# Attention scores over 128 rows: the low parts of the keys in their own tiles, padded with zeros

## The reference

```python
# first block, 8 heads
z = jnp.einsum('bhqd,bhkd->bhqk', q_blk, k_c) * scale
...
# second block, 16 heads
s = jnp.einsum('bhqd,bhkd->bhqk', q[:, :, lo:hi], k[:, :, :hi]).astype(jnp.float32) * scale
```

## Time and profile before

| | |
|---|---|
| median of 3 runs | 2132.58 us (2129.17 to 2135.8) |
| profiled execution, its own time | 2129.67 us |
| its span in the profile | 2127.9 us |
| mean granted TensorE clock | 0.992 |
| PE busy | 2082.2 us, 98% |
| DVE busy | 1106.3 us, 52% |
| ACT busy | 808.9 us, 38% |
| POOL busy | 111.9 us, 5% |

### The profile page before, as it was taken

How to read it: one execution, slowest core, us unless ns; L and a number is a source line. 1 busy time by engine, 2 the same in 40 slices (tenths; PEclk the granted TensorE clock), 3 DMA queues, 4 the chain that set the end, 5 groups by cost and what they waited for, 6 DMA issues and landing times.

```text
span 2127.9 us, 25125 instructions
## 1 busy us (share of the span) xinstructions
PE 2082.2 (98%) x10227; PEld 1720.3 (81%) x10227; DVE 1106.3 (52%) x1678; ACT 808.9 (38%) x1256; POOL 111.9 (5%) x131
## 2 busy tenths in 40 slices
PE   6999999999999999999999999999999999999997
PEld 4788888887778888888888887777888888888887
DVE  8734444576744554333335546564524476446546
ACT  4422222354544333222234445555323354234334
POOL 3100000100000010000011000000000100000012
PEclk8999999999999999999999999999999999999999
DMA  7734543443332313232222332222233222332241
GB/s 277 268 135 154 177 142 123 142 139 119 124 104 89 98 62 118 75 111 102 87 82 91 109 119 70 70 70 74 96 93 96 89 80 87 102 109 92 79 147 40
DMA packets 70165, 236.27 MB, mean 111 GB/s; under 512 B 7826, under 2 KB 10130, under 8 KB 69667
## 3 DMA queue, kind: packets, MB, share of 16 engines
q1 hardware_dynamic: 67874, 226.59, 32.2%
q0 software_dynamic: 2032, 7.90, 1.1%
q10 hardware_dynamic: 144, 0.18, 0.1%
HBM read 229.89 MB, written 4.75 MB: 110 GB/s over the span
## 4 chain that ended last, share of the span: by engine, by line
PE 92%; DVE 4%; ACT 2%; DMA 1%; issue 1%; POOL 0%; DVEq 0%; SPq 0%; ACTq 0%
PE bank L608 81%; PE bank L672 4%; PE bank L782 1%; PE bank L779 1%; PE bank L1012 1%; PE bank L894 1%; PE bank L998 1%; DVE w_lo L1570 1%; DVE raw_m L1566 0%; DMA w_raw<-in_w_mix_dram 0%; PE bank L924 0%; DVE kl L1759 0%; PE bank L987 0%; DVE ssq L1586 0%; PE bank L1044 0%
## 5 line engine op out<-in xcount | busy, mean ns | idle before, releaser
L1570 DVE TENSOR_TENSOR w_lo<-w_raw,w_hi 128x1024 fp32r<-128x1024 f32 (+2 forms) x367 | 418.2, 1167 | 217.0 <-ACT w_hi L1109 216.0
L608 PE MATMUL bank<-u_lo,w_hi 128*128 128x512 f32 (+1 forms) x1920 | 497.2, 371 | 11.2 <-DVE u_lo L1850 4.9
L608 PE MATMUL bank<-u_hi,w_hi 128*128 128x512 f32 (+1 forms) x1920 | 500.2, 373 | 6.7 <-ACT ple_s L1287 3.5
L608 PE MATMUL bank<-u_hi,w_lo 128*128 128x512 f32 (+1 forms) x1920 | 495.4, 371 | 0.0
L1109 ACT ACTIVATE w_hi<-w_raw 128x1024 fp32r<-128x1024 f32 (+2 forms) x368 | 347.4, 976 | 259.9 <-PE bank L608 195.5
L608 PEld LDWEIGHTS bank<-u_lo,w_hi 128*128 128x128 f32 x1920 | 357.1, 189 | 75.7 <-DVE u_lo L1850 5.7
L608 PEld LDWEIGHTS bank<-u_hi,w_hi 128*128 128x128 f32 x1920 | 358.9, 190 | 70.9 <-ACT ple_s L1287 3.9
L608 PEld LDWEIGHTS bank<-u_hi,w_lo 128*128 128x128 f32 x1920 | 357.2, 189 | 61.0 <-issue 2.3
L1688 DVE TENSOR_TENSOR ff_a<-ff_s,bank 128x512 f32<-128x512 f32 x44 | 30.2, 687 | 233.0 <-issue 220.2
L1183 ACT ACTIVATE act_hi<-ff_a 128x512 fp32r<-128x512 f32 x66 | 41.7, 632 | 256.7 <-DVE ff_a L1688 216.7
L608 PE MATMUL bank<-act_hi,w_lo 128*128 128x512 f32 (+1 forms) x561 | 131.1, 378 | 0.0
(11 more groups left out here) (270 smaller groups left out, 2126.4 us busy)
## 6 DMA issues: line engine op xcount, KB each, us to landing
w_raw<-in_w_gu_dram SPq DMA_DIRECT2D x127, 512.0 KB, 4.0
w_raw<-in_w_ada_dram SPq DMA_DIRECT2D x66, 512.0 KB, 4.5
w_raw<-in_w_dn_dram SPq DMA_DIRECT2D x48, 384.0 KB, 3.1
w_raw<-in_w_mix_dram SPq DMA_DIRECT2D x36, 512.0 KB, 3.6
w_raw<-in_w_dn_dram SPq DMA_DIRECT2D x48, 320.0 KB, 3.2
w_raw<-in_w_in_dram SPq DMA_DIRECT2D x24, 512.0 KB, 3.5
w_raw<-in_w_o_dram SPq DMA_DIRECT2D x16, 512.0 KB, 3.5
w_raw<-in_w_in_g_dram SPq DMA_DIRECT2D x16, 512.0 KB, 3.5
```

The lines of the kernel that those rows point to most:

```text
L608: m = e.matmul(bank[b][:, c], w, (x.lo if part == 2 else x.hi)[:, k, c], start=start, stop=stop, skip_group_check=True)
L1570: e.tensor_tensor(lo_of(name), raw_of(i), f32(hi_of(name)), ALU.subtract).then_inc(*s_w_lo.inc(name))
```

## The change

Each head of a pair gets its own tile for the low part of the keys (`kl_t[ph][s][p]`, eight tiles in all, four for each attention). The head's own 64 partitions are written by DVE as before; the other 64 are set to zero once for each attention by POOL (`zero_keys`). The second score product then reads the whole `qs` tile and the whole `kl` tile, 128 rows each: the rows in which `qs` holds the low part of the queries meet zeros. TensorE waits for the zeros (`s_kl_zero`) before a head's first product. To make room, `cv_y` is gone: the convolution accumulates in `yc_f` itself, and `cv_v` moves.

```diff
@@ tiles
-    kl_t = [ar(f"kl{s}", [P, T], F32R, 10 * s + 8) for s in range(2)]
+    kl_t = {ph: [[ar(f"kl{ph}{s}{p}", [P, T], F32R, 2 * s + at if p else 10 * s + 8) for p in range(2)] for s in range(2)]
+            for ph, at in (("a", 80), ("b", 44))}
...
-    cv_v = ar("cv_v", [P, T + 2], F32, 80)
-    cv_y = ar("cv_y", [P, T], F32, 82.5)
+    cv_v = ar("cv_v", [P, T + 2], F32, 84)
@@ TensorE
         def score(ph, out, c, p, queries, keys, keys_on_rows, start, stop):
-            s, own = c % 2, slice(64 * p, 64 * p + 64)
+            s = c % 2
+            q.wait_ge(s_kl_zero, (ph, s, p))
             q.wait_ge(s_q, (ph, c, 1))
             q.wait_ge(s_k, (ph, c, 1))
             a, k = qs_t[s][p][:, queries], ks_t[s][p][:, keys]
             l, r = (k, a) if keys_on_rows else (a, k)
             e.matmul(out, l, r, start=start, stop=False, skip_group_check=True)
-            a, k = qs_t[s][p][own, queries], kl_t[s][own, keys]
+            k = kl_t[ph][s][p][:, keys]
             l, r = (k, a) if keys_on_rows else (a, k)
             return e.matmul(out, l, r, start=False, stop=stop, skip_group_check=True)
@@ ScalarE, convolution
-                e.activation(cv_y[:, :], cv_v[:, 2:T + 2], ACT.Copy, scale=vec("conv_w", 8 + c)).then_inc(*s_cvy.inc(c))
+                e.activation(yc_f[:, c, :], cv_v[:, 2:T + 2], ACT.Copy, scale=vec("conv_w", 8 + c)).then_inc(*s_cvy.inc(c))
@@ VectorE, keys
-                e.tensor_tensor(kl_t[s][own, :], psum(key)[own, :], f32(ks_t[s][p][own, :]),
+                e.tensor_tensor(kl_t[ph][s][p][own, :], psum(key)[own, :], f32(ks_t[s][p][own, :]),
@@ VectorE, convolution
-                    e.scalar_tensor_tensor(cv_y[:, :], cv_v[:, k:k + T], vec("conv_w", 4 * k + c), cv_y[:, :], ALU.mult,
+                    e.scalar_tensor_tensor(yc_f[:, c, :], cv_v[:, k:k + T], vec("conv_w", 4 * k + c), yc_f[:, c, :], ALU.mult,
...
-                e.tensor_tensor(yc_f[:, c, :], cv_y[:, :], psum(key)[:, :], ALU.mult).then_inc(*s_yc.inc(c))
+                e.tensor_tensor(yc_f[:, c, :], yc_f[:, c, :], psum(key)[:, :], ALU.mult).then_inc(*s_yc.inc(c))
@@ GpSimd
+        def zero_keys(ph, key):
+
+            q.wait_ge(s_out, (key, 1))
+            for s in range(2):
+                for p in range(2):
+                    other = slice(64 - 64 * p, 128 - 64 * p)
+                    e.memset(f32(kl_t[ph][s][p][other, :]), 0.0).then_inc(*s_kl_zero.inc((ph, s, p)))
+                    q.wait_ge(s_kl_zero, (ph, s, p))
...
         last_squares("n1")
+        zero_keys("a", "1d17")
...
             add_square("n3", d, fold=True)
+        zero_keys("b", "2d17")
```

More of the change, by code:

```diff
@@ L352, in block_kernel @@
     arena = (cat + 63) // 64 * 64
-    assert base + arena + 86 * KB <= nc.sbuf_usable_end, base + arena + 86 * KB - nc.sbuf_usable_end
+    assert base + arena + 86 * KB + 32 <= nc.sbuf_usable_end, base + arena + 86 * KB - nc.sbuf_usable_end
     def ar(name, shape, dt, kb):
@@ L515, in block_kernel @@
     s_q_hi, s_q, s_k_hi, s_kl, s_k = signal("s_q_hi"), signal("s_q"), signal("s_k_hi"), signal("s_kl"), signal("s_k")
+    s_kl_zero = signal("s_kl_zero")
     s_v_act, s_v_dve = signal("s_v_act"), signal("s_v_dve")
```

## The result

The changed kernel takes 2107.47 us (median of 4 runs, 2105.64 to 2108.74), the kernel before 2131.39 (4 runs, 2129.17 to 2135.8, those shown above among them). The ratio is 0.9881, with a 95% interval of 0.9866 to 0.9896: 24 us, or 1.2%, faster. The forecast was 2108.5. The profiled execution took 2107.84 us, with a span of 2106.0 and a mean granted clock of 0.991.

What follows compares the result with a forecast made beforehand. PE was taken as the bound: 98% busy, 92% of the chain. 11.1 + 17.9 - 3.1 - 1.0 - 0.8 = 24.1 us saved, from the median 2132.58 to 2108.5 us; own range 2102 to 2114, chance 0.80.

Steps and rivals of the forecast that it cites:

- Phase a, 11.1 us: Phase a score bursts: seven heads save 1.47 us each, the first, which waits for `v_a`, 0.8; sum 11.1 us.
- Phase b, 17.9 us: Phase b score products: 64 steps save a mean of 0.28 us each, 17.9 us before anything is given back.
- Given back, 3.1 + 1.0 us: Phase b: 11 steps in five stretches off PE turn 3.1 us into wait; other turns with little slack, 1 us.
- POOL's zeros, 0.8 us: Boundaries before both phases: POOL's memsets may slow DVE's new input, so PE waits 0.4 us more at each.
- A: Phase b gives back 10 us instead of 4.1: 2114; with 2 us at each boundary 2118; chance 0.09.
- B: Score loads still wait because two products use the same rows; nothing saved, 2132.6 plus up to 2; chance 0.03.
- C: Score products: the switch is only half of the late load's cost, so 12 us are saved, 2120; chance 0.06.
- D: Half-clock stretches at phase b's 12 tiles and phase a's heads cost 34 us, 2142; decides from 14; chance 0.02.
- What would have shown the prediction wrong: Phase a bursts still over 2 us, phase b saving less than 10, or boundaries growing by over 1 us each.
- The dense layers kept 0.23 us from start to start: Sign in the profile after: matmuls of the dense layers still start 0.23 us apart.

Runs made afterwards that it cites:

- the kernel before with late low parts: Kernel before, with DVE writing the dense gate's low parts in phase b behind the next step's attention work: 2130.58 us, ratio 0.9983.
- the changed kernel with late low parts: Changed kernel, with DVE writing the dense gate's low parts in phase b behind the next step's attention work: 2102.45 us, ratio 0.9852.
- the grouped one: Kernel before, phase a's eight products per head reordered: four over 128 rows, then four over 64: 2124.57 us, ratio 0.9949.
- the third experiment: Kernel before, phase a's row-count switches cut from eight to two per head by reordering products, none widened: 2124.57 us, ratio 0.9949.

## Why the prediction was right

**Phase a, 11.1 us.** Measured 11.35, with a burst of 1.28 us where 1.26 was forecast. The pace of the sticks was the right row for a product not yet in the trace: same widths, same format, 128 rows. The other seven heads gained 1.48 us each, 10.36 in all (forecast 7 x 1.47 = 10.3). The first head gained 1.0 us, with a wait that grew by 0.28 us in it, where 0.8 was forecast, so nearly all of the term's error lies there.

**Phase b, 17.9 us.** Taken step by step, from the first score product to the second matmul after the mask, in the starts of the same matmuls, 64 steps save 17.35 us: 0.23 each with 128 columns (forecast 0.24), 0.28 with 256, 0.29 with 384 and with 512 (forecast 0.29). The term was 3% too large: each width saves up to 0.01 us less than forecast, and the mean of the four forecasts, 0.2775, had been rounded up to 0.28.

**Given back, 3.1 + 1.0 us.** 17.35 - 13.09 = 4.26 us, forecast 4.1; 3.56 of it stand as waits of PE, where about 4 were forecast. The size was right, but the picture behind it was only half so. I counted 11 score steps in five stretches off PE and let their saving turn into waits, which treats the stretches as fixed. They grew instead, from 37 to 67 us in all, since a shorter PE makes more of the steps depend on DVE. That the sum fits is in part luck: the return hangs in part on DVE's order of work, and moving 1.2 us of it took the return from 4.26 to 2.86 (17.35 - 14.49).

**POOL's zeros, 0.8 us.** The timeline of POOL before phase b, and the matmul that answers the earlier trace rows:

```profile
1140.88 2.25 POOL L2169 MEMSET klb<- 64x512 f32 x4 [5.36 <-PE bank L609]
```

```profile
1143.44 0.38 PE L609 MATMUL bank<-u_lo,w_hi 128*128 128x256 f32 x1 [1.00 <-DVE u_lo L1613]
```

Four memsets take 2.25 us. That is nearer to the memset of the earlier trace rows than to the sum of the earlier trace rows, as chosen. PE's wait grew from 0.88 to 1.00 us there, and from 0.49 to 0.72 before phase a, which looks like 0.35 us for the zeros. But the wait goes with the half-clock stretch at the boundary, not with the zeros. Before phase a it is 0.72 us in all five profiles with a stretch there and 0.49 in all four without. The first line below is of the kernel before with late low parts, which has no zeros; the second is of the changed kernel with late low parts, which has them:

```profile
425.92 0.39 PE L608 MATMUL bank<-u_lo,w_hi 128*128 128x256 f32 x1 [0.72 <-DVE u_lo L1615]
```

```profile
421.98 0.39 PE L609 MATMUL bank<-u_lo,w_hi 128*128 128x256 f32 x1 [0.49 <-DVE u_lo L1617]
```

Before phase b, in profiles without a stretch there, the wait is 1.00 us with zeros and 0.98 and 1.00 without (the kernel before with late low parts, and the grouped one). DVE's operations beside the memsets are no longer than in the kernels without zeros either: `ssq` takes 0.43 us, `hres` 0.48 to 0.49 and `u_lo` 0.42 to 0.48 in both kinds. So the zeros cost at most 0.02 us at a boundary, and the term of 0.8 was too large by all of it. Its reason, that POOL's writes might slow DVE, did not come about. No product waited for a zero.

**The rivals.** A did not come: 4.3 us were given back and not 10, and the zeros cost the boundaries nothing, not 4 us. B fell with the loads of the second head, which go ahead over the same 128 rows, against the rule quoted with it (the Trainium skill, TensorE: Matmul & The Clock Gate, Part 3: Packing small matmuls): here the trace disagrees with it. C fell with the result, 23.9 us and not 12; and the third experiment, with six switches fewer in each of eight heads, gives 8.03 / 8 / 6 = 0.17 us for each, near the 0.20 of the forecast, not half of it. D asked for 14 half-clock stretches; phase b has none, before or after, and its longest wait is 1.3 us.

What would have shown the prediction wrong did not come about: bursts under 2 us, phase b above 10, boundaries below 1. The dense layers kept 0.23 us from start to start. The errors were +0.25 us in phase a, -0.55 in the steps of b, -0.16 in the return and +0.8 in the zeros; they partly cancel and give the 24.4 us of the two phases, where 24.1 was forecast. Against the medians 23.9 us were gained. That this lies within 0.2 us of the forecast is luck too, since the interval of the ratio alone is 3 us to either side.

## What to carry to other kernels

Look in the loads' timeline for idle time that ends in "issue", not only at the matmuls: a load that goes out with its own matmul marks a switch, and in phase a each switch of the row count cost 0.17 to 0.20 us. Compare the load's start with its matmul's as well: behind products of 128 and 256 columns the idle time before a late load was only 0.07 to 0.13 us, and the view marks none of them. Remove switches by making the narrow product as wide as its neighbours with zeros, or, with no further tile, by grouping products of one row count (70% of phase a's gain). When PE gets shorter, read next what the engine behind its first wait does ahead of it, and move what is not urgent behind: here that was worth another 5 us, 3.65 of which could have been had in the kernel before.

## What the runs showed of the hardware

- A product over 64 rows is not slow by itself, and its loads go ahead when the product before has 64 rows too: four in 0.58 us. From the start of the last 128-row product with 512 columns to the first 64-row product, recorded with its bare load, it was 0.32 us, where 0.23 is the pace without a switch.
- The load of a bf16 product behind an fp32r product goes out late even though both use 128 rows, after 0.28 us without a load (1273.74 above). No experiment here changed its format, so what it would be worth in fp32r is open.
- A memset of 64x512 on POOL takes 0.56 us in a row of four, and did not slow DVE, which makes the new input at the same time: its operations took 0.42 to 0.49 us with and without memsets beside them.
- What sets off a half-clock stretch stays open. In the two profiles in which a wait of 1.9 us was covered the stretch behind it was gone, but waits of 1.2 us with one behind and 1.36 us without are both in these runs, and stretches at the boundaries came and went between kernels whose work there is the same.
